# A layer with 32 experts: token columns copied in SBUF by index in place of row gathers from DRAM, the residual kept in DRAM meanwhile

## The chip, the cores and the metric

One core of one Trainium2 chip runs the whole kernel. The metric is the device time of one execution in microseconds (us), the median of several runs. Matrix work is on TensorE (PE), element-wise work on VectorE (DVE) and ScalarE (ACT), GpSimd (POOL) issues indirect DMAs, and SyncE (SP) issues most of the other DMAs.

## The reference

One layer on x of 512 tokens by 1024 channels: a token mixer (stick-breaking attention and retention), cross-attention into 256 memory rows, a mixture of experts, and a last RMSNorm. The change lies in the mixture:

```python
logits = h @ w_router + b_router            # h = rmsnorm(x, g_moe), 512 x 1024
top_val, top_idx = lax.top_k(logits, 4)     # 4 of 32 experts for each token
gate = softmax(top_val)
# for each expert e and each of its tokens
hc  = h[token] @ w1[e] + b1[e]              # 1024 -> 2048
act = min(hc_glu, 7) * sigmoid(1.702 * ...) * (clip(hc_lin) + 1)
y   = act @ w2[e] + b2[e]                   # 1024 -> 1024
x[token] += gate * y
```

An expert's weights are 12 MB in float32, those of all 32 experts 384 MB. All of them are read once.

## The kernel before

**Up to the experts** the kernel runs projections, attention, retention and cross-attention. It ends with `res`, the residual stream of 512 tokens (`work` columns 8192 to 12288, 2 MB), and `h_nat`, its normalised rows with tokens on partitions. ACT stores `h_nat` into the DRAM tensor `h_rows` (`row_store`, L1007). The router's result is ranked on DVE, and PE runs idle matmuls meanwhile (`keep_running`, L1901).

**The experts** are taken in the order of their token counts, large and small alternating, from a table `order` in SBUF. A turn treats groups of 32 tokens: 3 groups (96 tokens) for experts 0, 1 and the even ones, 2 groups (64) for the odd ones (`CYCLE = (3, 2)`). An expert that has more tokens than that gets an overflow pass at the end, which these inputs do not use. The weights come in chunks of 1 MB, 12 for an expert: 8 for the first product (`up`, L1983) and 4 for the second (`down`, L2009). They go round 20 slots of SBUF. SP issues the load of a chunk (L530) as soon as PE has used the chunk that is in its slot (`w_used`), so SP is up to 20 chunks ahead.

The input of an expert must have channels on partitions (`x_t`). For expert 0 PE builds it with selection matrices from `h_nat` (L2076). For expert n from 1 on the steps are these:

- DVE compares the slots of all tokens with the table of places (`choose`, L1395), PE turns that into row numbers (`index`, L1920), and DVE writes them as integers (`idx`, L1426).
- POOL gathers the rows of `h_rows` by an indirect DMA into `xrows` (`gather_rows`, L687), 96 or 64 rows of 4 KB.
- PE transposes them (`x_turn`, L1941), and ACT copies the result out of PSUM (`x_keep`, L1031).

The order in a turn of PE is written out by hand:

```python
up(p, ...); x_turn(p + 1); spread(p - 1, ...); index(p + 2, ...); down(p - 1, ...); act_turn(p, ...)
```

DVE does `swiglu(p)` (L1526, L1530), waits for the gather `x_in`, and does `index`, `choose` and `now`. ACT does `gate_silu(p)` (L1039), `x_keep(p + 1)`, `y_evict(p - 1)` (L1051, L1052) and `act_keep(p)` (L1044). POOL scatters the outputs of an expert into the DRAM tensor `y_tok` (L726), 3 or 2 indirect DMAs of quarter rows.

**At the end** SP loads the 16 tiles of `y_tok` (L584), DVE adds them to `res` with the gates (L1580), and the last RMSNorm follows.

## Time and profile before

| | |
|---|---|
| median of 3 runs | 1755.39 us (1753.14 to 1755.88) |
| the profiled execution | 1752.49 us |
| its span on the core | 1750.8 us |
| mean granted clock of TensorE | 0.994 |
| PE busy | 1663.0 us (95%) |
| DVE busy | 451.3 us (26%) |
| ACT busy | 379.0 us (22%) |
| POOL busy | 184.9 us (11%) |
| read from HBM, written | 485.59 MB, 22.94 MB |
| queue q1 (SP's, weights) | 469.79 MB |
| queue q0 (POOL's) | 34.59 MB |

Busy time is the union of an engine's instructions; register and DMA-issuing instructions are not in it. A DMA share is the mean busy share of the core's 16 DMA engines in a stretch, and the GB/s are what they moved. The queue lines give packets, MB and the share of the 16 engines' time that the packets took. In a timeline each row has its start, its duration, the engine and line, the tile written and the tile read, the count, and in brackets how long the engine was idle before it and for what.

### The profile page before, as it was taken

Reading aid. Unit: us, or ns where it says so; the run is one execution under the profiler, and the core shown is the slowest. Engines: PE = TensorE matmul, PEld = TensorE weight load, DVE = VectorE, ACT = ScalarE, POOL = GpSimd, SP = SyncE. Lnnn points to the kernel's source line nnn. Section 1 sums busy time; section 2 is a strip of 40 time slices with the busy share of each in tenths; the row PEclk is TensorE's granted clock in tenths of the full one; section 3 lists DMA queues with packets and bytes.
Section 4 is the critical chain, followed back from the end, with each engine's and each line's share of the span. In section 5 each row is a group of like instructions: output and inputs, shape, how many; then the busy total and the mean of one; then the engine's idle time right before and its main releaser. Section 6 shows DMA issues by size and latency. Waiting matters only on the chain.

```text
span 1750.8 us, 36491 instructions
## 1 busy us (share of the span) xinstructions
PE 1663.0 (95%) x15752; PEld 936.6 (53%) x15752; DVE 451.3 (26%) x933; ACT 379.0 (22%) x596; POOL 184.9 (11%) x269
## 2 busy tenths in 40 slices
PE   7989999999999999999999999989899889899995
PEld 6766887888888867434344434424334334334331
DVE  4354526424645253521000100001001000010005
ACT  5564233433335333000000000000001000000001
POOL 0011301000000010011111111101101101111110
PEclk9999999999999999999999999999999999999999
DMA  7103634234225425799999999999999999999997
GB/s 257 61 25 91 219 124 160 73 96 168 97 74 203 180 81 218 310 372 391 398 411 401 408 399 410 401 412 409 404 411 406 405 412 403 409 411 402 413 415 286
DMA packets 98706, 508.71 MB, mean 291 GB/s; under 512 B 10650, under 2 KB 10834, under 8 KB 49056
## 3 DMA queue, kind: packets, MB, share of 16 engines
q1 hardware_dynamic: 86224, 469.79, 68.1%
q0 software_dynamic: 11760, 34.59, 6.0%
q8 instruction: 126, 2.06, 0.5%
q10 hardware_dynamic: 576, 2.10, 0.3%
q14 instruction: 20, 0.16, 0.0%
HBM read 485.59 MB, written 22.94 MB: 290 GB/s over the span
## 4 chain that ended last, share of the span: by engine, by line
PE 63%; SPq 19%; DMA 11%; issue 3%; DVE 3%; ACT 1%; POOL 0%; ACTq 0%; DVEq 0%; POOLq 0%
SPq L530 18%; PE ps L1983 15%; PE ps L1656 10%; PE ps L1657 10%; PE ps L1658 10%; PE ps L2009 8%; DMA moe<-in_w_exp_in 3%; DMA ring<-in_w_exp_in 3%; DMA ring<-in_w_exp_out 2%; PE ps L1752 1%; DMA ring<-y_tok 1%; PE ps L1799 1%; PE ps L1819 1%; PE ps L509 1%; PE ps L1941 1%
## 5 line engine op out<-in xcount | busy, mean ns | idle before, releaser
L1983 PE MATMUL ps<-ring,moe 128*32 128x512 f32 x3104 | 348.7, 597 | 23.8 <-DMA ring<-in_w_exp_in 23.8
L1526 DVE TENSOR_SCALAR moe<-ps 128x768 f32<-128x768 f32 (+1 forms) x32 | 26.7, 833 | 845.8 <-PE ps L1983 845.8
L1983 PEld LDWEIGHTS ps<-ring,moe 128*32 128x32 f32 x3104 | 92.6, 110 | 263.4 <-issue 202.6
L1122 DVE TENSOR_TENSOR wl<-raw,wh 128x1024 fp32r<-128x1024 f32 x102 | 123.6, 1224 | 230.1 <-ACT wh L787 230.1
L2009 PE MATMUL ps<-ring,moe 128*32 128x256 f32 x3136 | 174.0, 379 | 0.4 <-DMA ring<-in_w_exp_out 0.3
L1039 ACT ACTIVATE moe<-ps 128x768 f32<-128x768 f32 (+1 forms) x32 | 22.8, 711 | 641.8 <-DVE moe L1526 641.8
L1656 PE MATMUL ps<-oph,wh 128*128 128x512 f32 x384 | 151.1, 394 | 4.6 <-DVE opl L1157 2.2
L787 ACT ACTIVATE wh<-raw 128x1024 fp32r<-128x1024 f32 x102 | 106.8, 1061 | 222.5 <-PE ps L1658 222.5
L1657 PE MATMUL ps<-opl,wh 128*128 128x512 f32 x384 | 149.8, 390 | 0.0
L1658 PE MATMUL ps<-oph,wl 128*128 128x512 f32 x384 | 149.8, 390 | 0.0
L2009 PEld LDWEIGHTS ps<-ring,moe 128*32 128x32 f32 x3136 | 93.5, 110 | 71.5 <-DMA ring<-in_w_exp_out 1.5
L1983 PE MATMUL ps<-moe 128*32 128x512 f32 x1056 | 119.7, 593 | 7.8 <-DMA moe<-in_w_exp_in 7.7
L1983 PE MATMUL ps<-work,moe 128*32 128x512 f32 x1024 | 115.2, 594 | 11.0 <-DMA work<-in_w_exp_in 11.0
L726 POOL DMA_INDIRECT y_tok<-moe,spare x79 | 78.8, 997 | 256.8 <-ACT moe L1052 222.6
L1656 PE MATMUL ps<-wh,oph 128*128 128x512 f32 x248 | 97.5, 393 | 0.7 <-ACT work L845 0.7
L1657 PE MATMUL ps<-wl,oph 128*128 128x512 f32 x248 | 96.6, 389 | 0.0
L1658 PE MATMUL ps<-wh,opl 128*128 128x512 f32 x248 | 96.5, 389 | 0.0
L1656 PEld LDWEIGHTS ps<-oph,wh 128*128 128x128 f32 x384 | 72.4, 188 | 21.8 <-issue 6.0
L695 POOL CAST sel_c<-work 96x32 bf16 (+1 forms) x64 | 20.7, 349 | 581.8 <-DVE moe L1426 547.2
L1658 PEld LDWEIGHTS ps<-oph,wl 128*128 128x128 f32 x384 | 72.3, 188 | 15.3
L1983 PEld LDWEIGHTS ps<-moe 128*32 128x32 f32 x1056 | 31.1, 110 | 92.2 <-issue 69.6
L1657 PEld LDWEIGHTS ps<-opl,wh 128*128 128x128 f32 x384 | 72.4, 189 | 14.5
(302 smaller groups left out, 1811.1 us busy)
## 6 DMA issues: line engine op xcount, KB each, us to landing
ring<-in_w_exp_in SPq DMA_DIRECT2D x152, 1024.0 KB, 28.3
ring<-in_w_exp_out SPq DMA_DIRECT2D x78, 1024.0 KB, 29.2
moe<-in_w_exp_in SPq DMA_DIRECT2D x52, 1024.0 KB, 28.6
work<-in_w_exp_in SPq DMA_DIRECT2D x52, 1024.0 KB, 29.0
moe<-in_w_exp_out SPq DMA_DIRECT2D x26, 1024.0 KB, 28.2
raw<-in_w_in SPq DMA_DIRECT2D x25, 1024.0 KB, 5.4
work<-in_w_exp_out SPq DMA_DIRECT2D x24, 1024.0 KB, 28.3
y_tok<-spare POOLq DMA_DIRECT2D x16, 512.0 KB, 4.2
```

The lines of the kernel that those rows point to most:

```text
L530: sp.dma_start(held(s), expert_chunk(e, c)).then_inc(w_ring[s], 16)
L695: nc.gpsimd.tensor_copy(dst, exp_rows[0:96, bass.ds(e, 1)].to_broadcast([96, 32])).then_inc(sel_ready, 1)
L726: pool.indirect_dma_start(out=y_parts, out_offset=bass.IndirectOffsetOnAxis(ap=place_now[:, j:j + 1], axis=0), in_=y_sb[:, j, :], in_offse ...
L787: nc.scalar.activation(half_hi(g), raw[:, c % RAW, g % 2 * PC:(g % 2 + 1) * PC], ACT.Copy).then_inc(w_hi, 1)
L1039: nc.scalar.activation(glu_s[:, 0:g], ps[:, 0:g, 0:256].rearrange("p j (n a) -> p j a n", a=2), ACT.Silu, scale=ALPHA).then_inc(s_ready, 1)
L1122: nc.vector.tensor_tensor(half_lo(g), raw[:, g // 2 % RAW, g % 2 * PC:(g % 2 + 1) * PC], half_hi(g), ALU.subtract).then_inc(w_lo, 1)
L1526: nc.vector.tensor_scalar(act_n[:, 0:g], ps[:, 0:g, 256:512].rearrange("p j (n a) -> p j a n", a=2), 1.0 - LIMIT, 1.0 + LIMIT, ALU.max, AL ...
L1656: nc.tensor.matmul(o, a_hi_, b_hi_, start=start, stop=False)
L1657: nc.tensor.matmul(o, a_hi_, b_lo_, start=False, stop=False)
L1658: return nc.tensor.matmul(o, a_lo_, b_hi_, start=False, stop=stop)
L1983: ins = nc.tensor.matmul(ps[32 * s:32 * s + 32, j, :], xt[:, k, 32 * j:32 * j + 32], w[:, s, :, :], start=False, stop=(k == KT - 1), tile_ ...
L2009: ins = nc.tensor.matmul(y_bank(s, j), at[:, a, j, q, :], w[:, a, s, :], start=False, stop=(q == W2 - 1 and a == 1), tile_position=(0, 32 ...
```

## The change

Four things change.

1. **Columns instead of rows.** PE transposes all of `h_nat` (`column_turn`, 8 times 4 transposes), ACT copies the result to `h_cols`, 8 x 512 columns in the place of `res` (`column_tile`). For experts 2 to 31 `index` gets 8 more matmuls on PE, which give the token numbers as a row on one partition, and DVE writes them to `tok_row` (2 buffers). DVE then copies the first half of the columns and ACT the second half, one instruction for a token with a register in its address, 8 registers loaded at a time (`copy_tokens`). `x_t` has two buffers, so the copies for expert p+2 are made in turn p.
2. **Gone** for experts 2 to 31: the gather, `x_turn`, `x_keep`, and DVE's wait for `x_in`. Expert 1 keeps them.
3. **The residual waits in DRAM.** SP stores `res` into `r_rows` in two halves of 1 MB among the first weight loads, and loads it back (2 MB) after the last weight load, ahead of the tiles of `y_tok`. ACT waits for both stores before it writes `h_cols`; DVE waits for the load before its first sum.
4. **Idle matmuls gone.** The two `keep_running` calls (24 matmuls) make way for the 32 transposes. The last 8 of them wait until ACT has copied the first four tiles, and `index(0)` waits for all eight tiles.

```diff
@@ copy_tokens, new
+        def x_t(g, b):
+            return m_(1024 - 1024 * b, KT * 32 * g).rearrange("p (k n) -> p k n", k=KT)
+        h_cols = w_(8192, KT * T).rearrange("p (k n) -> p k n", k=KT)
+        def copy_tokens(engine, copy, n, lo, hi):
+            b = n % 2
+            for s in range(lo, hi, 8):
+                _, tokens = nc.values_load_multi_w_load_instructions(
+                    tok_row[b][:, s:s + 8], engines=[engine], min_val=0, max_val=T - 1,
+                    skip_runtime_bounds_check_because="the row is clamped to the last token when it is written")
+                for i, token in enumerate(tokens):
+                    ins = copy(x_t(CYCLE[b], b)[:, :, s + i:s + i + 1], h_cols[:, :, bass.ds(token, 1)])
+            return ins
@@ SP
+                if s in (13, 15):
+                    half = (s - 13) // 2
+                    sp.wait_ge(tile_out["dve"], slabs[f"co{half}"].out0 + 4)
+                    sp.dma_start(r_rows[:, :, 512 * half:512 * half + 512], res[:, :, 512 * half:512 * half + 512]).then_inc(res_moved, 16)
...
             load(final, EC - 1, (CHUNKS - 1) % SLOTS)
+            sp.wait_ge(x_dve, NE - 2)
+            sp.wait_ge(x_act, NE - 2)
+            sp.dma_start(res, r_rows).then_inc(res_moved, 16)
@@ POOL
-            def step(p, old, e, g):
-                pool.wait_ge(xt_made, p + 2)
-                pool.wait_ge(idx_out, p + 2)
+            def step(p, i, old, e):
+                pool.wait_ge(row_ready, p + 1)
                 pool.wait_ge(sel_used, p + 1)
                 pool.sem_inc(bias_turn, 1)
                 bias_on(old, e)
-                gather_rows(g)
@@ ACT
+            act.wait_ge(res_moved, 32)
+            for k in range(KT - 2):
+                column_tile(k)
             act.preload_act_table_set("natural_log_exp_and_others")
...
+            for k in range(KT - 2, KT):
+                column_tile(k)
...
-            def step(p, m, i):
+            def step(p, m, i, more=True):
                 gate_silu(p, CYCLE[i])
-                x_keep(p + 1, CYCLE[1 - i])
                 y_evict(p - 1, CYCLE[i - 1], p * EC + (DOWNS - EC))
                 act_keep(p, CYCLE[i])
+                if more:
+                    act.wait_ge(row_ready, p + 1)
+                    act.sem_inc(bias_turn, 1)
+                    copy_tokens(mybir.EngineType.Activation, lambda out, in_: nc.scalar.activation(out, in_, ACT.Copy), i,
+                                16 * CYCLE[i], 32 * CYCLE[i]).then_inc(x_act, 1)
@@ DVE
                 swiglu(p, CYCLE[i], p * EC + UPS)
-                dve.wait_ge(x_in, p * 16 + 16)
-                index(p + 2, CYCLE[i], i)
+                index(p + 2, CYCLE[i], i, row=True)
                 e = expert_at(p + 3)
                 choose_with(e, e, CYCLE[1 - i])
                 now(p - 1, g, stores)
+                copy_part(p + 2, i)
@@ PE
-            keep_running(18)
+            pe.wait_ge(nat_ready, TT)
+            for k in range(KT - 2):
+                column_turn(k)
...
+                    for t in range(TT):
+                        for c in range(2):
+                            nc.tensor.matmul(ps[0:1, 3, 64:64 + 32 * g], column[:, t, c, 0:1], pick[:, t, 0:32 * g],
+                                             start=(t == 0 and c == 0), stop=(t == TT - 1 and c == 1), skip_group_check=True)
...
-            keep_running(6)
+            pe.wait_ge(ht_out, KT + 4)
+            for k in range(KT - 2, KT):
+                column_turn(k)
...
+                    pe.wait_ge(x_dve, n - 1)
+                    pe.wait_ge(x_act, n - 1)
...
                 up(p, CYCLE[i], p * 2 + 1)
-                x_turn(p + 1)
                 spread(p - 1, groups(p - 1), p - 1, p + 2, (p + 1) % 2)
                 if to_index:
-                    index(p + 2, CYCLE[i])
+                    index(p + 2, CYCLE[i], row=True)
                 down(p - 1, groups(p - 1), p * 2)
-                act_turn(p, CYCLE[i], p + 2)
+                act_turn(p, CYCLE[i])
```

The lists below are the built program's instructions in their order. This is PE between the products of two experts, before:

```order
L1983 MATMUL ps<-work,moe 32x512 x48
L1941 MATMUL ps<-ident,moe 128x96 x8
L1930 MATMUL ps<-spare,ident 32x2 x8
L1920 MATMUL ps<-spare,moe 96x2 x12
L2000 MATMUL ps<-bias_b,sel_c 32x256 x8
L2009 MATMUL ps<-ring,moe 32x256 x32
L2009 MATMUL ps<-moe 32x256 x32
L1951 MATMUL ps<-ident,moe 128x128 x6
```

and the same place in the changed kernel:

```order
L2056 MATMUL ps<-work,moe 32x512 x48
L2056 MATMUL ps<-ring,moe 32x512 x24
L2056 MATMUL ps<-moe 32x512 x24
L1996 MATMUL ps<-spare,ident 32x2 x8
L1982 MATMUL ps<-moe,spare 1x96 x8
L1986 MATMUL ps<-spare,moe 96x2 x12
L2073 MATMUL ps<-bias_b,sel_c 32x256 x8
L2082 MATMUL ps<-ring,moe 32x256 x64
L2020 MATMUL ps<-ident,moe 128x128 x6
```

The eight transposes of gathered rows (L1941) are gone; eight matmuls with one output row (L1982) stand ahead of the twelve of `index` (L1986).

This is ACT in one turn of an expert with 3 groups, before:

```order
L1039 ACTIVATE moe<-ps 128x768
L1031 ACTIVATE moe<-ps 128x768
L1051 ACTIVATE moe<-ps 128x256
L1052 ACTIVATE moe<-ps 128x512
L1044 ACTIVATE moe<-ps 128x768
```

and now, with the first columns of its half:

```order
L1076 ACTIVATE moe<-ps 128x768
L1088 ACTIVATE moe<-ps 128x256
L1089 ACTIVATE moe<-ps 128x512
L1081 ACTIVATE moe<-ps 128x768
L523 TENSOR_LOAD moe
L1063 ISA
L1063 ACTIVATE moe<-work 128x8
L1063 ISA
L1063 ACTIVATE moe<-work 128x8
```

`x_keep` (L1031) is gone. Behind `act_keep` (L1081) stands one register load for eight columns (L523), and for each column an instruction on registers (ISA) and the copy of 8 elements on 128 partitions (L1063); with 3 groups ACT has 6 such loads and 48 copies, with 2 groups 4 and 32. DVE has as many.

This is SP before the experts in the changed kernel, where the two stores of the residual (L569) stand:

```order
L547 DMA ring<-in_w_exp_in 128x2048 [waits w_used]
L547 DMA ring<-in_w_exp_in 128x2048
L569 DMA r_rows<-work 128x4x512 [waits tile_out_dve]
L547 DMA moe<-in_w_exp_in 128x2048 [waits w_used]
L547 DMA moe<-in_w_exp_in 128x2048
L569 DMA r_rows<-work 128x4x512 [waits tile_out_dve]
L547 DMA work<-in_w_exp_out 128x2048 [waits lg_done,nat_ready]
L547 DMA work<-in_w_exp_out 128x2048
L547 DMA work<-in_w_exp_out 128x2048 [waits xt_made,h_stored]
```

The first store stands behind the second load of a pair, the other behind the last load whose slot the projections held; the loads with "waits xt_made,h_stored" follow.

## Rows read from the trace of the kernel before

**Rows 1.** The page, part 2: busy tenths of the DMA engines in 40 slices.

```profile
DMA  7103634234225425799999999999999999999997
```

**Rows 2.** Timeline of PE (start, duration, engine, line, tiles): the starts of four even experts.

```profile
836.72 0.83 PE L1974 MATMUL ps<-bias_b,sel_c 96*32 96x512 bf16 x12
...
1070.06 0.83 PE L1974 MATMUL ps<-bias_b,sel_c 96*32 96x512 bf16 x12
...
1129.25 0.83 PE L1974 MATMUL ps<-bias_b,sel_c 96*32 96x512 bf16 x12
...
1648.91 0.83 PE L1974 MATMUL ps<-bias_b,sel_c 96*32 96x512 bf16 x12
```

**Rows 3.** Timeline of PE in two turns: a wait inside up, and x_turn.

```profile
1302.20 1.92 PE L1983 MATMUL ps<-ring,moe 128*32 128x512 f32 x16 [0.69 <-DMA ring<-in_w_exp_in]
...
1346.43 0.88 PE L1941 MATMUL ps<-ident,moe 96*128 96x96 f32 x8
```

**Rows 4.** DMA queues in 1465 to 1480 us: packets, MB, share of 16 engines.

```profile
q1 hardware_dynamic: 866, 6.30, 101.0%
```

**Rows 5.** Timeline of POOL from 1480 us: the gathers of one pair.

```profile
1480.69 1.01 POOL L687 DMA_INDIRECT moe<-h_rows,moe  x1 [0.27 <-issue]
...
1511.07 0.99 POOL L687 DMA_INDIRECT moe<-h_rows,moe  x1 [0.15 <-issue]
```

**Rows 6.** DMA queues in 1515 to 1521 us, a gather for 64 rows landing.

```profile
q1 hardware_dynamic: 259, 1.90, 88.6%
q0 software_dynamic: 80, 0.21, 11.9%
```

**Rows 7.** DMA queues in 1484 to 1491 us, a gather for 96 rows landing.

```profile
q1 hardware_dynamic: 306, 2.22, 88.2%
q0 software_dynamic: 112, 0.28, 13.0%
```

**Rows 8.** DMA queues in 1524 to 1533 us, three scatters landing.

```profile
q1 hardware_dynamic: 473, 3.46, 92.1%
```

**Rows 9.** DMA queues in 1129.25 to 1648.91 us, eight pairs of experts.

```profile
q8 instruction: 49, 0.80, 0.6%
...
moe<-h_rows,moe POOLq DMA_INDIRECT x16
```

**Rows 10.** Stretches of time: busy of each engine, granted clock, DMA share, GB/s.

```profile
685.00:690.00 5.00, 5.00 (x27) 4.20 (x26) 2.62 (x4) 2.17 (x6) 0.00 (x0) 1.00 0.00 0
740.00:745.00 5.00, 5.00 (x40) 1.47 (x36) 4.86 (x5) 0.00 (x0) 0.00 (x0) 0.78 1.03 362
760.00:770.00 10.00, 10.00 (x196) 5.64 (x192) 2.78 (x8) 1.51 (x2) 1.71 (x3) 1.00 0.89 320
```

**Rows 11.** Timeline of all engines where the experts begin.

```profile
689.45 0.80 SPq L530 DMA_DIRECT2D moe<-in_w_exp_in  x2
...
695.73 0.60 ACT L1016 ACTIVATE work<-ps 128x512 f32<-128x512 f32 x1 [1.14 <-PE ps L1885]
...
703.95 7.38 PE L2076 MATMUL ps<-moe,work 128*128 128x96 f32 x64
...
711.37 0.81 ACT L1031 ACTIVATE moe<-ps 128x768 f32<-128x768 f32 x1 [9.87 <-PE ps L2076]
...
716.48 0.16 DVE L1463 CAST work<-moe 1x15 uint32<-1x15 f32 x1
...
721.13 0.96 SPq L530 DMA_DIRECT2D ring<-in_w_exp_in  x2
```

**Rows 12.** Timeline of ACT and DVE: short instructions, and a register load ahead of one.

```profile
691.55 0.21 ACT L1003 ACTIVATE small<-small 128x4 f32<-128x4 f32 x1 [0.65 <-DVE small L1354]
...
1349.56 0.15 DVE L1429 COPY spare<-ps 96x2 f32<-96x2 f32 x1
...
1721.73 1.28 ACT L1097 ACT_TABLE_LOAD   x1 [0.20 <-issue]
```

**Rows 13.** Timeline at the end: the sums wait for the expert rows.

```profile
1720.32 5.48 DVE L1580 SCALAR_TENSOR_TENSOR work<-ring,work 128x1024 f32<-128x1024 f32 x4 [6.93 <-DMA ring<-y_tok]
```

More of the change, by code:

```diff
@@ L429, in layer_kernel @@
         zero_x = sem("zero_x")
+        res_moved = sem("res_moved")
+        row_ready, x_dve, x_act = (sem(n) for n in ("row_ready", "x_dve", "x_act"))
         pickl_ready, gl_made, gl_kept, own_done = (
@@ L1024, in _, with copy_part, x_keep @@
                 ins.then_inc(gate_exp, 1)
+            for k in range(KT - 2, KT):
+                column_tile(k)
             act.preload_act_table_set("silu_and_others")
-            def x_keep(n, g):
-                act.wait_ge(xt_made, n + 1)
-                nc.scalar.activation(x_t(g).rearrange("p (b k) n -> p b k n", b=2),
+            def copy_part(n, b):
+                act.wait_ge(row_ready, n - 1)
+                copy_tokens(mybir.EngineType.Activation, lambda out, in_: nc.scalar.activation(out, in_, ACT.Copy), b,
+                            16 * CYCLE[b], 32 * CYCLE[b]).then_inc(x_act, 1)
+            def x_keep(made, g, b):
+                act.wait_ge(xt_made, made)
+                nc.scalar.activation(x_t(g, b).rearrange("p (b k) n -> p b k n", b=2),
                                      ps[:, 6:8, 0:4 * CAP].rearrange("p b (k n) -> p b k n", k=4)[:, :, :, 0:32 * g], ACT.Copy).then_inc(xt_kept, 1)
@@ L1086, in _ @@
                     step(m * 2 + (2 + i), m, i)
-            step(NE - 2, CYCLES - 1, 0)
+            step(NE - 2, CYCLES - 1, 0, more=False)
             last_step(NE - 1)
@@ L1933, in spread, with x_turn @@
                 ins.then_inc(spread_done, 1)
-            def x_turn(n, first=False):
-                pe.wait_ge(x_in, n * 16)
-                if not first:
-                    pe.wait_ge(at_kept, n - 1)
+            def x_turn(landed, kept=None):
+                pe.wait_ge(x_in, landed * 16)
+                if kept is not None:
+                    pe.wait_ge(at_kept, kept)
                 for k in range(KT):
@@ L1943, in x_turn, with act_turn @@
                 ins.then_inc(xt_made, 1)
-            def act_turn(n, g, after):
+            def act_turn(n, g, after=None):
                 pe.wait_ge(act_ready, n + 1)
-                pe.wait_ge(xt_kept, after)
+                if after is not None:
+                    pe.wait_ge(xt_kept, after)
+                else:
+                    pe.wait_ge(at_kept, n)
                 for h in range(2):
@@ L1963, in chunk_in, with up @@
                 return held(c)
-            def up(n, g, sel, first=False, over=None, between={}):
-                pe.wait_ge(xt_kept, n + 1)
+            def up(n, g, sel, first=False, over=None, between={}, kept=None):
+                if kept is not None:
+                    pe.wait_ge(xt_kept, kept)
+                else:
+                    pe.wait_ge(x_dve, n - 1)
+                    pe.wait_ge(x_act, n - 1)
                 if not first:
@@ L1977, in up @@
                     ins.then_inc(sel_used, 1)
-                xt = x_t(g)
+                xt = x_t(g, 0 if over is not None else n % 2)
                 for k in range(KT):
@@ L2079, in _ @@
             pe.wait_ge(b_hi, 3)
+            pe.wait_ge(ht_out, 2 * KT)
             index(0, groups(0))
-            up(0, groups(0), 1, first=True, between={1: lambda: index(1, groups(1))})
-            x_turn(1, first=True)
-            index(2, CYCLE[0])
+            up(0, groups(0), 1, first=True, between={1: lambda: index(1, groups(1))}, kept=1)
+            x_turn(1)
+            index(2, CYCLE[0], row=True)
             act_turn(0, groups(0), 2)
-            up(1, groups(1), 3)
-            x_turn(2)
+            up(1, groups(1), 3, kept=2)
             spread(0, groups(0), 0, 3, 0)
-            index(3, CYCLE[1])
+            index(3, CYCLE[1], row=True)
             down(0, groups(0), 2, first=True)
-            act_turn(1, groups(1), 3)
+            act_turn(1, groups(1))
             def step(p, i, to_index=True):
                 up(p, CYCLE[i], p * 2 + 1)
-                x_turn(p + 1)
                 spread(p - 1, groups(p - 1), p - 1, p + 2, (p + 1) % 2)
                 if to_index:
-                    index(p + 2, CYCLE[i])
+                    index(p + 2, CYCLE[i], row=True)
                 down(p - 1, groups(p - 1), p * 2)
-                act_turn(p, CYCLE[i], p + 2)
+                act_turn(p, CYCLE[i])
             for p in range(2, NE - 2):
@@ L2108, in _ @@
             up(NE - 1, CYCLE[1], 2 * NE - 1)
-            act_turn(NE - 1, CYCLE[1], NE)
+            act_turn(NE - 1, CYCLE[1])
             last_down()
@@ L2121, in _ @@
                         spread(j + NE, GR, j + (NE - 1), j + (NE + 1), 0, 2)
-                        x_turn(j + NE)
-                        up(j + NE, GR, j * 2 + (2 * NE + 1), over=j)
-                        act_turn(j + NE, GR, j + (NE + 1))
+                        x_turn(j + 2, j + (NE - 1))
+                        up(j + NE, GR, j * 2 + (2 * NE + 1), over=j, kept=j + 3)
+                        act_turn(j + NE, GR, j + 3)
                         down(j + NE, GR, j * 2 + (2 * NE + 2), over=j)
```

70 lines of the change are left out of this document (45 added, 25 removed).

## The prediction, made before any run of the changed kernel

> **What bounds the kernel now.** I read the page first. From slice 18 of 40 on, where the experts are under way, the DMA engines stand at nine tenths or more but for the last slice [rows 1]. So the question is whether PE or the weight stream sets the pace. The timeline of PE answers it in two parts. The even experts start at 836.72 and, four pairs on, at 1070.06 us: 58.3 us a pair, with PE never idle. From 1129.25 to 1648.91 us eight pairs pass: 65.0 us a pair [rows 2], and inside `up` PE waits some 0.6 us for nearly every chunk [rows 3]. A pair of experts reads 24 chunks of 1.049 MB, 25.17 MB. The DMA engines move this at their full share all the time; at first PE lives on the 20 chunks that were loaded ahead and eats this lead at 6.7 us a pair, then it goes at the stream's pace. The bound is the DMA stream. PE has 6.7 us of slack in each pair.
>
> What does the stream do with its time? Where nothing but weights moves, q1 gets 6.30 MB through in 15 us, 0.420 MB/us [rows 4]. At this rate 24 chunks take 59.9 us, and a pair takes 65.0. The missing 5.1 us are what POOL's indirect DMAs and the instruction fetch take. The change removes one of the two indirect kinds, the gathers.
>
> **The gathers, removed.** POOL issues one in each turn [rows 5]; its rows land some 4 to 10 us later. In the 6 us of a gather of 64 rows q1 moves 1.90 MB where 2.52 would go: 0.62 MB less, 1.5 us [rows 6]. In the 7 us of one of 96 rows it moves 2.22 of 2.94 MB, 1.7 us less [rows 7]. The gathered bytes alone are 0.21 and 0.28 MB, 0.5 and 0.7 us, so more than their bytes is lost: q1's share falls to 88.6% while its bytes fall to 75% of what the clean rate gives. The mean is 1.6 us a gather, 3.2 us a pair. As a cross-check, three scatters cost 3.78 - 3.46 = 0.32 MB, 0.8 us [rows 8]; two I put at 0.5; the fetch is 0.6% of 65.0, 0.4 us [rows 9]. Of the 5.1 us this leaves 3.4 for the two gathers, 1.7 each.
>
> There are 30 such gathers (16 in the eight pairs, [rows 9]). The two for experts 2 and 3 fall in a stretch in which the stream is short of free slots anyway: between 760 and 770 us the DMA share is 0.89 [rows 10]. Their removal gives nothing. The other 28 give 28 x 1.6 = 44.8 us. In the first pairs a turn with 3 groups frees slots more slowly than the emptier queue fills them, so a little goes unused: I take off 3 us by choice (0 to 10). **Gain: 42 us.**
>
> Does PE let it through? The new pair takes 65.0 - 3.2 = 61.8 us, against 58.3 of PE. PE also loses `x_turn`, 0.88 us a turn [rows 3], and gets 8 matmuls with one output row, which I put between nothing and that same row of 8 matmuls; they even out at worst. PE's own chain from 836.72 would reach expert 30, 13 pairs on, at 1595; the stream brings it there at 1648.91 - 42 = 1607. PE stays hidden, by 12 us: the end of the experts is still the stream's.
>
> **The copies on DVE and ACT, added.** Each engine copies 48 and 32 columns in a pair, with 10 loads of 8 registers. No row shows such a copy. From below: the shortest ACT instruction here takes 0.21 us, two DVE copies of a few elements start 0.06 to 0.07 us apart and take 0.15, and a register load ahead of ACT's table load leaves 0.20 us idle [rows 12]. So ACT needs 48 x 0.21 + 6 x 0.20 = 11 us for the large expert, DVE less. From above: six single register loads of SP lie between DVE's 716.64 us (716.48 + 0.16) and SP's first refill at 721.13 [rows 11], 0.75 us each. If each of the 8 registers cost that, a column would cost 0.96 us. I take 0.21 to 0.30 us a column, as a load of eight is one instruction; the nearest row is ACT's own. ACT's copies start behind `act_keep(p)`, beside `up(p+1)`. `gate_silu(p+1)` stands behind them, and it is needed before `act_turn(p+1)`, which comes after `up(p+1)` and `down(p)`: eight chunks of 2 groups at 1.92 us [rows 3] are 15 us, and `down(p)` with 3 groups is a good sixth of PE's pair of 58.3 us, 10 us: 25 us in all. 48 columns fit up to 0.5 us each. The products `up(p+2)` that need them come a whole turn later. Cost: 0. If the cover goes, the price is that of the rival below.
>
> A page has a price for the loads. The Trainium skill, "Runtime: NRT & Kernel Launch", Instruction fetch mechanics, states that a TENSOR_LOAD takes about 200 ns for each register even in bulk; by that a column costs 0.41 us, 48 of them 20 us, still under the cover, and the sum is unchanged. No row here shows a load of eight.
>
> DVE's and ACT's longer programs are fetched too: some 350 instructions a pair beside PE's 1600 or so, at a total fetch share of 0.6% now [rows 9]. I put 1 us on it (0 to 2).
>
> **The start, moved.** The first store of `res` goes out where the DMA engines stand still: share 0.00 from 685 to 690 us [rows 10]. Free. The second goes behind the two loads of 689.45 us [rows 11]: 2.1 MB, 5 us; itself 1.05 MB, 2.5 us; and ACT's own stores of `h_rows` share the engines from 693 us on. I expect it landed near 702 (698 to 705). ACT waits for that behind its copy of 695.73 us, while PE's ranking and DVE do not. Then ACT copies six tiles at 0.6 us, loads its table, does the gates (2 us), two tiles, a table of 1.28 us: 10 us, so it is ready for `x_keep(0)` near 712, against 711.37 now. PE's last 8 transposes wait for four tiles (704.5), so the product of expert 0 begins near 706 in place of 703.95 and takes 7.4 us [rows 11]. Both put the first `up` 1 to 3 us later, and with it the table of the order and the first refill. As the stream runs dry there already, this passes on in full: +3 us (0 to 5). The idle matmuls are gone: after a stop of PE the granted clock reads 0.78 in 740 to 745 us [rows 10]; a like dip over the product of expert 0 costs +1 us (0 to 3).
>
> **The end, moved.** The load of `res`, 2.1 MB, goes in between the last weights and the tiles of `y_tok` in the same queue. The engines are full there, and DVE's first sum waits 6.93 us for such a tile at 1720.32 us [rows 13]. So all tiles come 2.1/0.42 = 5 us later: +5 us (4 to 6).
>
> **The sum.** -42 + 1 + 3 + 1 + 5 = -32 us. The profiled execution took 1752.5 us, so 1720.5; the median of the runs, 2.9 us above it, goes to **1723.4 us**. Its own bounds: with 1.7 us a gather, nothing lost early and the small ends of the rest 47.6 - 4 = 43.6 us less, 1711.8; with 1.4 us a gather, 10 lost early and the large ends 29.2 - 16 = 13 us less, 1742.
>
> **The rivals.**
>
> *A gather costs its bytes only.* The dips of q1 in [rows 6, 7] would then come from something else that stands in the same place. Its 0.245 MB at 0.42 MB/us are 0.58 us, 28 of them 16 us; with the 10 us of the other terms the gain is 6 us: 1749. For it: a row is 4 KB, long against the other packets. Against it: three scatters, with as many bytes and smaller pieces, lose 0.8 us together, about their bytes, in windows that differ only in what POOL sent. The Trainium skill, "DMA: Bandwidth & Descriptors", Specifications, gives 512 bytes as the least transfer at line rate; by that rule a gathered row of 4 KB costs its bytes and this rival holds. The trace disagrees with it here, 1.5 us against 0.5.
>
> *The copies become the bound, and the kernel is slower.* The place is ACT between `act_keep(p)` and `gate_silu(p+1)`. ACT's work in a pair is 80 columns and some 4 us of its other copies. Once a column costs more than (65.0 - 4)/80 = 0.76 us, ACT takes longer than the pair does now and PE waits for `act_ready` and `x_act`. At the upper price of 0.96 us a pair takes 81 us, 16 more, over 14 pairs 224: with the other terms about 1990. Against it: no short instruction on ACT takes a third of this. For it: the price of a register load in eights, and of an address that waits for it, is not in the trace.
>
> *The change does not free the stream.* If SP's issuing rather than the engines limited q1, the weights would not move up. The terms at start and end would stay: 1765. Against it: the share is 101.0% with weights alone [rows 4].
>
> **How the numbers follow.** Forecast 0.78, bytes only 0.11, copies bound 0.07, stream not freed 0.04. A measurement of this kernel can tell 0.2%, 3.5 us. Bytes only is mostly faster (1749) and partly no change. Faster 0.87, same 0.03, slower 0.10. The range is the forecast's own, 1711 to 1742; what lies outside is the three rivals, 0.22, less the better half of the first, which may reach into it.
>
> **What would show it.** Right: pairs of 61 to 62.5 us late in the experts, q1 near 0.42 MB/us but for the scatters; ACT's copies at 0.2 to 0.3 us and idle before `gate_silu`; the first refill at 721 to 726 us; the tiles of `y_tok` 5 us later behind the weights. Wrong: late pairs near 64 (bytes only), PE waiting for ACT or DVE at `up` or `act_turn` (copies bound), or a first refill after 730 us.

## The result, and the profile after

| | before | after |
|---|---|---|
| median | 1755.45 us (1753.14 to 1755.88, 4 runs) | 1723.4 us (1720.73 to 1726.49, 4 runs) |
| profiled execution, span | 1752.49, 1750.8 us | 1724.01, 1722.2 us |
| read from HBM, written | 485.59, 22.94 MB | 477.86, 25.03 MB |
| queue q0 (POOL's) | 34.59 MB | 26.70 MB |
| DVE, ACT busy | 451.3, 379.0 us | 613.2, 510.4 us |

The ratio of after to before is 0.9821, interval 0.9802 to 0.9840: 32 us less, where 32 were forecast.

The page of the changed kernel, part 2 (40 slices of 43 us) and part 3 (queue, packets, MB, share of 16 engines):

```profile
GB/s 249 74 25 61 228 125 173 89 98 159 86 98 192 199 3 243 248 386 369 412 418 420 419 421 419 420 419 420 419 420 419 420 420 419 420 420 418 419 402 263
...
q1 hardware_dynamic: 87808, 473.99, 68.7%
q0 software_dynamic: 8880, 26.70, 4.6%
...
q14 instruction: 29, 0.24, 0.0%
```

From slice 21 to slice 38 the engines now move 418 to 421 GB/s without a dip. The timeline of PE shows the starts of even experts (start us, duration, engine, line, tiles), the same matmuls as [rows 2]:

```profile
840.87 0.83 PE L2047 MATMUL ps<-bias_b,sel_c 96*32 96x512 bf16 x12
...
1069.87 0.83 PE L2047 MATMUL ps<-bias_b,sel_c 96*32 96x512 bf16 x12
...
1304.22 0.83 PE L2047 MATMUL ps<-bias_b,sel_c 96*32 96x512 bf16 x12
...
1427.49 0.83 PE L2047 MATMUL ps<-bias_b,sel_c 96*32 96x512 bf16 x12
...
1489.92 0.83 PE L2047 MATMUL ps<-bias_b,sel_c 96*32 96x512 bf16 x12
...
1614.02 0.83 PE L2047 MATMUL ps<-bias_b,sel_c 96*32 96x512 bf16 x12
```

The early pairs take (1069.87 - 840.87)/4 = 57.25 us, PE's own pace (58.3 before). For the late ones the same five pairs are compared, those that end with expert 30. In the kernel before they begin here:

```profile
1324.48 0.83 PE L1974 MATMUL ps<-bias_b,sel_c 96*32 96x512 bf16 x12
```

They take (1614.02 - 1304.22)/5 = 61.96 us now and took (1648.91 - 1324.48)/5 = 64.89 before. Expert 30 starts 34.9 us earlier than before. The queues in one late pair, of 62.43 us:

```profile
q1 hardware_dynamic: 3514, 25.58, 98.6%
q0 software_dynamic: 240, 0.51, 2.1%
q8 instruction: 6, 0.10, 0.6%
```

And in 15 us with hardly anything but weights (1470 to 1485 us), beside [rows 4]:

```profile
q1 hardware_dynamic: 858, 6.24, 100.4%
```

ACT in a large turn (timeline; in brackets the idle time before the row and for what). The copies come in eights, with one load of 8 registers between:

```profile
1459.05 0.96 ACT L1108 ACTIVATE moe<-work 128x8 f32 x8
1460.48 0.97 ACT L1108 ACTIVATE moe<-work 128x8 f32 x8 [0.46 <-issue]
...
1466.28 0.97 ACT L1108 ACTIVATE moe<-work 128x8 f32 x8 [0.46 <-issue]
1478.53 0.60 ACT L1076 ACTIVATE moe<-ps 128x512 f32<-128x512 f32 x1 [11.27 <-DVE moe L1572]
```

DVE likewise:

```profile
1454.86 1.06 DVE L527 COPY moe<-work 128x8 f32 x8 [0.58 <-issue]
```

An octet and its load take (0.97 + 0.46)/8 = 0.18 us a column on ACT and (1.06 + 0.58)/8 = 0.205 us on DVE. `gate_silu` (L1076) waits 11.27 us for DVE's result with ACT idle: the copies stand in nobody's way.

The start, in the timelines of all engines, beside [rows 11]:

```profile
690.20 0.81 SPq L547 DMA_DIRECT2D moe<-in_w_exp_in  x2
...
691.42 0.38 SPq L569 DMA_DIRECT2D r_rows<-work  x1
...
705.52 3.05 ACT L1044 ACTIVATE work<-ps 128x512 f32<-128x512 f32 x6 [8.44 <-DMA r_rows<-work]
...
707.64 1.97 PE L1957 MATMUL ps<-ident,work 128*128 128x128 f32 x8 [4.48 <-ACT work L1044]
709.40 8.10 PE L2150 MATMUL ps<-moe,work 128*128 128x96 f32 x64
...
717.54 0.81 ACT L1068 ACTIVATE moe<-ps 128x768 f32<-128x768 f32 x1 [4.16 <-PE ps L2150]
...
727.65 0.61 SPq L547 DMA_DIRECT2D ring<-in_w_exp_in  x2
```

ACT stands 8.44 us for the second store, PE 4.48 us for ACT, and the product of expert 0 takes 8.10 us in place of 7.38. The windows (busy time of each engine, granted clock, DMA share, GB/s) show why the latter, and what it costs the stream:

```profile
705.00:710.00 5.00, 2.36 (x12) 2.36 (x12) 4.64 (x9) 4.45 (x8) 0.00 (x0) 0.50 1.03 431
710.00:715.00 5.00, 5.00 (x42) 5.00 (x41) 0.00 (x0) 3.36 (x11) 0.00 (x0) 0.89 0.08 33
715.00:720.00 5.00, 4.60 (x59) 3.58 (x61) 1.93 (x5) 0.81 (x1) 0.95 (x1) 1.00 0.29 69
```

PE was stopped, and the granted clock reads 0.50 (1.2 of 2.4 GHz) at first and 1.00 from 715 us. The DMA engines meanwhile have nothing to do (0.08 and 0.29): all slots are full and the first refill waits for PE. It comes at 727.65 us against 721.13 before.

The end, the loads of SP and the first sum of DVE, beside [rows 13]:

```profile
1657.49 2.13 SPq L604 DMA_DIRECT2D work<-r_rows  x1
...
1667.03 29.13 SPq L608 DMA_DIRECT2D ring<-y_tok  x16
...
1690.32 1.28 DVE L1631 SCALAR_TENSOR_TENSOR work<-ring,work 128x1024 f32<-128x1024 f32 x1 [12.30 <-DMA ring<-y_tok]
```

From expert 30's start to the end of the span pass 1722.2 - 1614.02 = 108.2 us, against 1750.8 - 1648.91 = 101.9 before: 6.3 more. The first sum of DVE starts 76.3 us after expert 30, against 71.4 before: 4.9 of the 6.3. The other 1.4 come behind it. PE adds some tiles of `y_tok` with their gates, 8 matmuls for a tile of tokens. Here are the first 8 before, then the same 8 in the changed kernel, for which DVE waits:

```profile
1725.58 3.70 PE L2055 MATMUL ps<-ring,moe 128*128 128x512 f32 x8 [2.01 <-DMA ring<-y_tok]
```

```profile
1696.21 6.05 PE L2128 MATMUL ps<-ring,moe 128*128 128x512 f32 x8 [5.04 <-DMA ring<-y_tok]
...
1702.29 1.23 DVE L1643 TENSOR_TENSOR work<-ps,work 128x1024 f32<-128x1024 f32 x1 [0.87 <-PE ps L2128]
```

PE had waited 5.04 us, and the granted clock reads 0.50 from 1695 to 1700 us; in the kernel before it waited 2.01 us and the clock reads 1.00 from 1722 to 1732 us. So 0.87 of the 1.4 us belong to the clock.

### The profile page after: what moved, and what is told of

It reads as the page before. It is cut to its first block, busy times and chain, and to the rows that moved or that the text cites. A ratio compares the mean times of both kernels' runs of the same rounds, so it can differ in the third digit from the quotient of the medians.

```text
span 1722.2 us, 41426 instructions
## 1 busy us (share of the span) xinstructions
PE 1645.5 (96%) x15736; PEld 933.0 (54%) x15736; DVE 613.2 (36%) x2133; ACT 510.4 (30%) x1774; POOL 151.4 (9%) x239
## 3 DMA queue, kind: packets, MB, share of 16 engines
q0 software_dynamic: 8880, 26.70, 4.6%
HBM read 477.86 MB, written 25.03 MB: 292 GB/s over the span
## 4 chain that ended last, share of the span: by engine, by line
PE 69%; SPq 17%; DMA 8%; issue 3%; DVE 2%; ACT 1%; POOL 0%; POOLq 0%; DVEq 0%; ACTq 0%
PE ps L2056 18%; SPq L547 16%; PE ps L1708 10%; PE ps L1709 10%; PE ps L1710 10%; PE ps L2082 10%; DMA moe<-in_w_exp_out 2%; DMA ring<-in_w_exp_in 2%; DMA moe<-in_w_exp_in 2%; PE ps L1804 1%; DMA ring<-y_tok 1%; PE ps L1851 1%; PE ps L1871 1%; DMA r_rows<-work 1%; PE ps L515 1%
## 5 line engine op out<-in xcount | busy, mean ns | idle before, releaser
L2056 PEld LDWEIGHTS ps<-ring,moe 128*32 128x32 f32 x3104 | 94.5, 110 | 245.6 <-issue 205.7
L527 DVE COPY moe<-work 128x8 f32 x1200 | 161.6, 178 | 82.4 <-issue 81.5
L1108 ACT ACTIVATE moe<-work 128x8 f32 x1072 | 131.6, 205 | 53.0 <-issue 53.0
L1076 ACT ACTIVATE moe<-ps 128x768 f32<-128x768 f32 (+1 forms) x32 | 22.7, 711 | 411.7 <-DVE moe L1572 411.7
L2082 PEld LDWEIGHTS ps<-ring,moe 128*32 128x32 f32 x3136 | 95.2, 110 | 70.1 <-issue 1.4
```

The lines of the kernel that those rows point to most:

```text
L527: ins = copy(x_t(CYCLE[b], b)[:, :, s + i:s + i + 1], h_cols[:, :, bass.ds(token, 1)])
L1108: copy_tokens(mybir.EngineType.Activation, lambda out, in_: nc.scalar.activation(out, in_, ACT.Copy), i, 16 * CYCLE[i], 32 * CYCLE[i]).the ...
L2056: ins = nc.tensor.matmul(ps[32 * s:32 * s + 32, j, :], xt[:, k, 32 * j:32 * j + 32], w[:, s, :, :], start=False, stop=(k == KT - 1), tile_ ...
L2082: ins = nc.tensor.matmul(y_bank(s, j), at[:, a, j, q, :], w[:, a, s, :], start=False, stop=(q == W2 - 1 and a == 1), tile_position=(0, 32 ...
```

## The experiments

Beside these runs the kernel before had medians of 1754.0 to 1755.5 us. Differences below are between medians, unless said otherwise.

### The gathers

**The gathers back, into other partitions.** The 28 gathers of experts 4 to 31 are issued in POOL's order as before; nobody uses the rows. DVE writes the row numbers for them again and waits for each gather, as it did before.

```diff
@@ POOL, in the step of a turn
+                    pool.wait_ge(idx_out, p + 2)
...
+                    pool.indirect_dma_start(out=spare[32:32 + 32 * CYCLE[i], 0:D], out_offset=None, in_=h_rows,
+                                            in_offset=bass.IndirectOffsetOnAxis(ap=idx[0:32 * CYCLE[i], :], axis=0),
+                                            bounds_check=T - 1, oob_is_err=False).then_inc(x_in, 16)
```

> The changed kernel, and POOL also gathers the rows of experts 4 to 31 as before, into an unused part of SBUF; nobody uses them. Theory (a gather takes 1.6 us of the weight stream, more than its bytes): 28 gathers give back about 42 us, so near 1765 us, and late pairs of experts go back from 62 to 65 us. Rival (a gather costs its bytes, 0.58 us): 16 us, near 1739 us, pairs of 63 us. Rival (the gain came from the shorter PE turn without the 8 transposes): no change from 1723 us.

Measured: 1750.16 us (1747.9 to 1752.88), ratio to before 0.9978 (0.9968 to 0.9987), 26.8 us above the changed kernel: 0.96 us a gather, between the two theories. The rival that the gain came from the shorter turn of PE falls, since PE's turn is as short as in the changed kernel.

**The kernel before without its gathers.**

```diff
-                gather_rows(g)
...
-                pe.wait_ge(x_in, n * 16)
+                pe.wait_ge(x_in, 16)
...
```

DVE's waits for `x_in` are lowered in the same way.

> The kernel before, without the gathers of experts 2 to 31; the transposes stay and take the rows of expert 1 each time, so these experts compute on wrong tokens. Theory: the stream's gain alone, without the costs at start and end: 42 us less than before, near 1713 us, pairs of 62 us. Rival (bytes only): 16 us less, near 1739 us.

Measured: 1714.45 us, ratio 0.9777 (0.9761 to 0.9793), 39.6 us below the kernel before that was measured beside it; expert 30 starts at 1611.31. The forecast's first term was 42. The transposes of PE stand here as before, so the whole gain comes from the gathers, and the other parts of the change give some 9 us of it back (1723.4 against 1714.45). By the trace of the changed kernel start and end cost more, 12.8 us; here the first `up` itself starts 2.0 us later than before (714.28), and the other 2 us are not explained.

**Plain rows in place of gathers.** The same number of rows of `h_rows`, without an index.

```diff
-                gather_rows(g)
+                pool.dma_start(xrows[0:32 * g, :], h_rows[0:32 * g, :]).then_inc(x_in, 16)
```

> The kernel before, but each gather for experts 2 to 31 is a plain DMA on the same queue of the first 96 or 64 rows of h_rows into the same place: the same bytes, the same row length, the same target, no index; these experts compute on wrong tokens. If the loss of the weight stream lies in the shape (rows of 4 KB into single partitions), it stays: near 1755 us. If it lies in the indexed DMA itself, only the bytes are left: 28 times 1.0 us less, near 1729 us.

Measured: 1765.08 us, ratio 1.0064 (1.0047 to 1.0081): 11 us slower than with the gathers. q0 moves 36.53 MB in place of 34.59, since a gather leaves out the rows of empty places. The index is not what costs.

**The gathers back, into the partitions of before.** The first two experiments left a contradiction: the same 28 gathers are worth 39.6 us in the kernel before and 26.8 in the changed one. One difference is where the rows land: partitions 0 to 95 and 0 to 63 before, 32 to 127 and 32 to 95 in the first experiment.

```diff
@@ against the first experiment
-                    pool.indirect_dma_start(out=spare[32:32 + 32 * CYCLE[i], 0:D], out_offset=None, in_=h_rows,
+                    pool.indirect_dma_start(out=spare[0:32 * CYCLE[i], 0:D], out_offset=None, in_=h_rows,
```

> The changed kernel with the 28 gathers of experts 4 to 31 back in POOL's order, as in the run that cost 26.8 us, but with their rows put into partitions 0 to 95 or 0 to 63, as before, and not into 32 to 127 or 32 to 95. Theory (the partitions decide how much a gather costs, and the 1.5 us each that the change won came with the low ones): about 40 us slower than the changed kernel, 1763, and more weight packets of 0.65 us than in that run. Rival (the partitions do not matter; a gather in this place costs 0.95 us): 1748 to 1752.

Measured: 1763.4 us (1762.95 to 1766.62), ratio 1.0058 (1.0043 to 1.0074). 40.0 us above the changed kernel, as the theory has it: 1.43 us a gather, and 13 us more than with the other partitions. The DMA queues show which gathers differ. All windows are 8 us long. First the experiment with partitions from 32 up: without a gather (1430 to 1438 us), with one of 96 rows (1412 to 1420), with one of 64 rows (1441 to 1449):

```profile
q1 hardware_dynamic: 464, 3.38, 101.3%
```

```profile
q1 hardware_dynamic: 363, 2.64, 89.5%
q0 software_dynamic: 112, 0.28, 11.1%
```

```profile
q1 hardware_dynamic: 420, 3.06, 92.5%
q0 software_dynamic: 80, 0.22, 6.9%
```

And the experiment with partitions from 0 up, a gather of 64 rows (1451 to 1459 us):

```profile
q1 hardware_dynamic: 378, 2.74, 91.6%
q0 software_dynamic: 80, 0.22, 9.3%
```

At 3.38 MB in 8 us (0.4225 MB/us) the 96 rows take 0.74 MB from the weights, 1.75 us. 64 rows into partitions 0 to 63 take 0.64 MB, 1.5 us; 64 rows into 32 to 95 take 0.32 MB, 0.76 us, not far above the 0.22 MB of their own. The single packets say it more sharply. A weight packet of 8192 bytes takes 0.31 us. Counted over the trace's packets, while a gather of 96 rows lands or one of 64 rows into partitions 0 to 63, mostly 60 to 100 of them take over 0.4 us, in the kernel before as in this one. While 64 rows land in partitions 32 to 95, 0 to 2 do, in all 14 such gathers. A scatter, which reads SBUF, has 0 to 3 late in the experts.

The windows are a little high. Over the five last pairs the run from partition 32 up takes (1641.13 - 1321.09)/5 = 64.01 us and the one from 0 up (1653.63 - 1329.38)/5 = 64.85, which is 2.05 and 2.89 us above the changed kernel, where the windows add up to 2.5 and 3.25. The difference between the two runs, 0.84 us a pair, is near the windows' 0.75.

So the partitions are shown to set the price of a gather of 64 rows: the two kernels differ in this one line. For 96 rows both places, 0 to 95 and 32 to 127, cost the same 1.75 us, and that their excess has the same cause is argued and not shown. The Trainium skill, "SBUF — State Buffer", SBUF: two separate sides (the DMA port swizzle), has a rule that fits: of SBUF's 16 DMA ports, partitions 0 to 63 reach eight and 64 to 127 the other eight. By it 64 rows from partition 0 all press on one half, 96 rows load the halves 64 to 32 from either end, and only 32 to 95 is even; it says nothing of the weights beside them, but the trace agrees in all four cases. An estimate by it: 64 rows of 4 KB through half of 0.42 MB/us are 0.26/0.21 = 1.25 us, evenly 0.62; the windows show 1.5 and 0.76. For 96 rows the fuller half has 64 too, so by this estimate they cost 1.25 as well, while the windows show 1.75. An even split of 96 rows (48 and 48) was not tried.

### The start and the end

**No store of `res`.** `x` is loaded at the end in place of the stored residual.

```diff
-                if s in (13, 15):
-                    half = (s - 13) // 2
-                    sp.wait_ge(tile_out["dve"], slabs[f"co{half}"].out0 + 4)
-                    sp.dma_start(r_rows[:, :, 512 * half:512 * half + 512], res[:, :, 512 * half:512 * half + 512]).then_inc(res_moved, 16)
...
-            act.wait_ge(res_moved, 32)
-            sp.dma_start(res, r_rows).then_inc(res_moved, 16)
+            sp.dma_start(res, x[0].rearrange("(t p) d -> p t d", p=P)).then_inc(res_moved, 16)
```

> The changed kernel without the two stores of the residual and without ACT's wait for them; at the end x is loaded in the residual's place (the same 2 MB), so the output lacks the mixer's and the attention's part. Theory: the wait for the second store costs some 5.4 us at the start of the experts and passes on in full: near 1718 us, first refill near 722 us in place of 727.7, and no fall of TensorE's granted clock at the product of expert 0. Rival (the stream's lead hides a late start): within 1 us of 1723.

Measured: 1720.39 us (1718.56 to 1720.41), 3.0 less, with the first refill at 723.51 us. PE's product starts at 705.99 and takes 7.38 us again; the weight loads ahead of it were issued 1.29 us later than in the changed kernel (691.49 against 690.20), a drift from before the experts. Taken from that issue on, the first `up` starts 22.8 us later without the stores (714.27) and 28.2 us with them (718.40). The stores cost 5.4 us at this place; the drift of 1.29 us and another 1.1 us are missing in the total.

**The second store by tiles, ahead of two weight loads.**

```diff
-                if s in (13, 15):
...
+                if s == 13:
+                    sp.wait_ge(tile_out["dve"], slabs["co0"].out0 + 4)
+                    sp.dma_start(r_rows[:, :, 0:512], res[:, :, 0:512]).then_inc(res_moved, 16)
+                    for t in range(TT):
+                        sp.wait_ge(tile_out["dve"], slabs["co1"].out0 + t + 1)
+                        sp.dma_start(r_rows[:, t, 512:D], res[:, t, 512:D]).then_inc(res_moved, 16)
```

> The changed kernel, but the second store of the residual goes out tile by tile as each is done, and ahead of the two weight loads that stood before it. Theory: the stores land near 695 us in place of 705, ACT waits for nothing, the first product comes 5 to 6 us earlier and so does the end: near 1718 us. Rival (the stores only push the h_rows stores and the weights back): no change.

Measured: 1718.85 us (1717.23 to 1720.57), 4.6 less: nearly all that the stores cost. The product starts at 704.39 us with full clock.

**No load of `res` at the end.**

```diff
-            sp.dma_start(res, r_rows).then_inc(res_moved, 16)
```

> The changed kernel without the load of the residual at the end: the last sums add to whatever stands in its place, so the residual is missing from the output. Theory: 2 MB less in a full queue ahead of the tiles of y_tok: 5 us less, near 1718 us. Rival (the tiles wait for the last scatter anyway): no change.

Measured: 1717.87 us (1713.79 to 1718.54), 5.5 less; 5 were put on it.

**The load in four tiles among the tiles of `y_tok`.**

```diff
-            sp.dma_start(res, r_rows).then_inc(res_moved, 16)
+            sp.dma_start(res[:, 0, :], r_rows[:, 0, :]).then_inc(in_x[0], 16)
             for u in range(TT * TOPK):
+                if u in (4, 8, 12):
+                    sp.dma_start(res[:, u // 4, :], r_rows[:, u // 4, :]).then_inc(in_x[u // 4], 16)
```

> The changed kernel, but the residual is loaded back in four tiles, each just ahead of the four tiles of y_tok that it is summed with. Theory: the first sum can begin 3.7 us earlier, since only 0.5 MB stands before its first tile in place of 2 MB, and DVE's chain from there is as long as before: 3 us less, near 1720 us. Rival (the chain on DVE and PE waits for the later tiles instead): 0 to 1 us.

Measured: 1721.75 us (1721.1 to 1725.06), 1.7 less where the theory has 3. The first sum starts at 1686.72 us, 3.6 us earlier as foreseen, but the later sums wait for their tiles, one of them 2.47 us at 1696.07, which is the rival's mechanism. The times of this run and of the changed kernel overlap, so the 1.7 us by themselves are inconclusive.

**Both.** The early store and the load by tiles together, with the lines of the two diffs above.

> The changed kernel with both edits of the residual's way: the second half of the store by tiles and ahead of two loads of weights, and the reload in four tiles between the tiles of y_tok. Theory (the start and the end add up): the 4.6 us of the first edit and the 1.7 us of the second, about 6 us less than the changed kernel, 1717. Rival (the start comes early only to lose at the end, since the stream still sets the time of expert 30 and of the reload): no more than the first edit alone, 1719.

Measured: 1716.28 us (1715.1 to 1717.98), ratio to before 0.9785 (0.9772 to 0.9799), 7.1 less than the changed kernel; by the ratios, 0.0036 of 1755, 6.3 us. The first `up` starts at 713.10, expert 30 at 1609.14, 4.9 us earlier, and from there to the end of the span (1714.6) pass 105.5 us in place of 108.2. Start and end add up. Of the kernels here that copy the tokens this is the fastest.

### The copies

**All columns on ACT.** This was to test whether the split matters, with ACT twice as busy and still covered.

```diff
-                            16 * CYCLE[b], 32 * CYCLE[b]).then_inc(x_act, 1)
+                            0, 32 * CYCLE[b]).then_inc(x_act, 1)
...
-                copy_tokens(mybir.EngineType.DVE, nc.vector.tensor_copy, b, 0, 16 * CYCLE[b]).then_inc(x_dve, 1)
+                dve.sem_inc(x_dve, 1)
```

> The changed kernel, but ACT copies all columns and DVE none. At 0.18 us a column ACT needs 17 us for a large expert and 11.5 for a small one, 29 of 62 us in a pair. Theory (25 us of cover behind act_keep): no change from 1723 us. Rival (the halves were needed): PE waits at act_turn or up, pairs over 62 us.

Measured: 1751.56 us (1748.52 to 1754.1, 10 runs), 28 more than the changed kernel. The theory fell, though its reasoning about ACT held. The timeline of ACT, large turn:

```profile
1368.02 0.96 ACT L1108 ACTIVATE moe<-work 128x8 f32 x8 [0.46 <-issue]
1372.29 0.60 ACT L1076 ACTIVATE moe<-ps 128x512 f32<-128x512 f32 x1 [3.30 <-DVE moe L1572]
```

ACT is done 3.30 us before it is needed. PE waits for weights. The page, part 2, and the queues of one pair (1319.3 to 1383.7 us):

```profile
GB/s 245 73 25 76 232 125 160 72 97 168 90 80 193 192 70 232 289 371 390 418 418 419 418 419 418 419 415 405 417 404 407 412 390 400 406 397 394 406 370 222
```

```profile
q1 hardware_dynamic: 3499, 25.48, 97.6%
q0 software_dynamic: 240, 0.53, 2.1%
q8 instruction: 6, 0.10, 0.7%
q14 instruction: 5, 0.04, 0.1%
```

The stream itself is slower from slice 27 on, pairs take (1577.20 - 1190.85)/6 = 64.4 us, and a queue that is silent in the changed kernel moves 5 packets of 8 KB of instructions in each pair. Two runs were to tell what did it.

**ACT's loop only made longer.** The split of the change, but waits that are met at once ahead of the copies.

```diff
+                    for _ in range(16 * CYCLE[i] * 9 // 4):
+                        act.wait_ge(w_first, 16)
                     copy_tokens(mybir.EngineType.Activation, lambda out, in_: nc.scalar.activation(out, in_, ACT.Copy), i,
```

> The changed kernel with its own split of the columns; ACT's loop body only made longer, by 108 and 72 waits on a semaphore that was raised long before (180 instructions a pair, about what the 80 further columns added in the run with all on ACT). They read no tensor and load no register. Theory (the length of the body costs, since its instructions are brought again in each round): ACT's instruction queue moves some 80 to 90 packets in place of 29, late pairs take over 63.5 us, about 1750 us. Rival (the 80 further register loads and copies themselves disturb the stream, the length does not): 29 packets or few more, late pairs at 62, 1722 to 1727 us.

Measured: 1750.72 us (1749.8 to 1752.35, 10 runs), 27.3 more. The page, part 2, and the same stretch:

```profile
GB/s 245 73 25 80 230 124 160 72 97 168 97 73 196 189 73 233 273 382 392 419 418 418 419 418 419 419 414 407 416 402 408 405 395 403 406 396 407 405 376 215
```

```profile
q14 instruction: 5, 0.04, 0.2%
```

Slice by slice this is nearly the run with all columns on ACT. The waits read no tensor and load no register, so neither is needed for the loss; longer code in ACT's loop is enough. The waits also take time: the copies of a large turn begin some 4 us later behind `act_keep` than in the changed kernel. No run separates this delay from the length of the code, but PE waits for nothing except weights here too.

**All columns on DVE.**

```diff
-                copy_tokens(mybir.EngineType.Activation, lambda out, in_: nc.scalar.activation(out, in_, ACT.Copy), b,
-                            16 * CYCLE[b], 32 * CYCLE[b]).then_inc(x_act, 1)
+                act.sem_inc(x_act, 1)
...
-                copy_tokens(mybir.EngineType.DVE, nc.vector.tensor_copy, b, 0, 16 * CYCLE[b]).then_inc(x_dve, 1)
+                copy_tokens(mybir.EngineType.DVE, nc.vector.tensor_copy, b, 0, 32 * CYCLE[b]).then_inc(x_dve, 1)
```

> The changed kernel, but DVE copies all columns of an expert and ACT none: the mirror of the run with all on ACT, which cost 28 us though ACT fitted. It tells whether that cost belongs to a long loop body or to ACT. Theory (a loop body that has grown by two instructions a column, 80 columns a pair, and a load per eight, is brought from DRAM again in every round, and these reads slow the weight packets): DVE's body grows by the same number, its instruction queue moves more packets than now, some weight packets take about 0.65 us in place of 0.31, late pairs take 63.5 to 65 us, about 1750 us. Rival (the cost is ACT's alone): late pairs stay at 62 and the time at 1722 to 1728. The copies themselves, 80 more columns of 0.205 us in a pair, are 16 us a pair and fit in DVE's idle time by both.

Measured: 1773.34 us (1770.95 to 1776.98), ratio 1.0117 (1.0102 to 1.0133), 50 more. Its page:

```profile
q14 instruction: 85, 0.70, 0.1%
```

So it is not ACT's alone, and PE again waits for nothing but weights. With nearly the same number of packets as on ACT the cost is almost double, and pairs take (1596.69 - 1198.70)/6 = 66.3 us; the theory had 1750. What a longer loop costs on which engine is measured here; why the price differs is open.

## Why the prediction was right, point by point

- **The gathers, 42 us.** Expert 30 came 34.9 us earlier although the stream started 6.5 us later, 41.4 us by the stream. Without gathers the kernel before gained 39.6, and 28 gathers put back cost 40.0. The mechanism was right: a gather takes about three times its bytes from the stream. The price was read a little high. Five late pairs are 64.89 - 61.96 = 2.93 us shorter each, 1.47 a gather where the windows gave 1.6, and 28 x 1.47 is 41. The 3 us that were taken off by choice for the first pairs made up for it, and that is luck. The cause, which the prediction left open, is for 64 rows the partitions that they are written to.
- **The rival that a gather costs its bytes** falls, with its 1749 us. It comes near for one kind, 64 rows into partitions 32 to 95, which the kernel before does not have. The Trainium skill, "DMA: Bandwidth & Descriptors", Specifications, gives 512 bytes as the least transfer at line rate. That is no guide to the price here: 64 rows of 4 KB cost 1.4 times their bytes (0.32 for 0.22 MB) or 2.9 times (0.64), by their partitions.
- **PE hidden.** PE was put at 58.3 us a pair and 12 us of cover. It took 57.25: `x_turn` went, 1.76 us a pair, and the row matmuls took back 1.76 - 1.08 = 0.7. From 840.87 us PE's chain would reach expert 30 at 840.87 + 13 x 57.25 = 1585, so the cover was 29 us.
- **The copies, 0.** 0.18 us a column on ACT and 0.205 on DVE, below the 0.21 to 0.30 that were taken. The rival in which the copies bound falls: it began at 0.76. The Trainium skill, "Runtime: NRT & Kernel Launch", Instruction fetch mechanics, gives 200 ns for each register, and the trace does not agree for eights from SBUF: the load of 8 registers leaves 0.46 us idle on ACT and 0.58 on DVE, some 0.06 to 0.07 a register.
- **The instruction fetch, 1 us** for the longer programs: in the changed kernel the share stayed at 0.6% of q8 and q14 was silent, so it cost nothing that can be seen. But this term was sized by bytes, and that is the weak step of the prediction: had the copies all stood on one engine, it would have been 28 or 50 us. That the halves keep both loops short was luck to the forecast.
- **The start, 3 + 1 us,** was sized too low: 6.5 (727.65 against 721.13), outside the 721 to 726 that were named. The step that was off is the landing of the second store. It was put at 702, which left some 4 us for sharing the engines with ACT's stores of `h_rows`, and it ended just before ACT's first copy at 705.52, at the late end of 698 to 705. From 698 to 706 us ACT's stores (queue q10) moved 1.84 MB and q1 only 1.50. From there the prediction's own chain holds: PE's product 4 us behind the landing, 709.40 us in place of 706. The lower clock on the product cost 0.7 where 1 was put. From the issue of the loads (690.20 against 689.45) on it is 5.8 us, and the experiments give the stores 5.4 of it: 4.7 of waiting and 0.7 of the lower clock.
- **The end, 5 us:** 6.3 by the trace, 5.5 by the experiment without the load. The first sum comes 4.9 us later, as forecast. The prediction looked for a fall of the clock at the start alone; the second one, at the end, makes up 0.9 of the rest.
- **The sum.** -41.4 + 6.5 + 6.3 = -28.6 us, and the two profiled executions stand 1752.49 - 1724.01 = 28.5 apart, where the prediction had 32: start and end cost 2.5 and 1.3 us more than they were given, the gathers brought 0.6 less, the fetch took back its 1. The profiled execution of before lies 3.0 us below its median and that of after 0.6 above, so the medians are 32 apart. So the profiled execution was missed by 3.5 us (1720.5 against 1724.01), and that the forecast meets the median to a tenth is chance. The mechanism is shown, and each term is within 2.5 us.

## What to carry to other kernels

When a DMA stream at full rate is the bound, the price of another transfer is what the stream loses while it lands, read over a window of the queue's bytes, and here it was up to three times the transfer's own bytes. For 64 rows, moving them to the partitions 32 to 95 halved it; try that before removing the transfer. Count the instructions of a loop body too: the longer bodies here showed as packets in every round on an instruction queue that was silent before, and as a slower stream, not as a wait for that engine. When an engine's wait is moved into a serial start, follow it to the engine that waits for it in turn, and to the clock that this engine loses.

## What the runs showed of the hardware that was not expected

- 64 rows of 4 KB into partitions 32 to 95 cost the weight stream 0.76 us, into 0 to 63 1.5 us; 28 gathers moved by 32 partitions, 13 us of the whole.
- ACT's loop body longer by 180 waits: 27.3 us of 1723, with 5 packets of 8 KB (0.04 MB) more in each pair. At 0.42 MB/us these are 0.1 us a pair, while the pair takes 64.4 - 62 = 2.4 us more. The weight packets of 8192 bytes are the ones that slow down (from 1319.3 to 1383.7 us 69 of 3086 take over 0.4 us, and 6 of 3223 in the changed kernel), mostly not at the time of the instruction packets. The packets come in every pair from about 910 us on, but the stream slows only from about 1140 us, so such packets alone do not slow it. How the two hang together is open.
- In the changed kernel q14 has no packet between 907 and 1570 us, some 11 pairs, though ACT and DVE go round their loops: they need nothing new. In the runs with the longer bodies it has 5 packets in every pair. The other instruction queue, q8, brings 6 packets of 16 KB in every pair in all of them. The Trainium skill, "Runtime: NRT & Kernel Launch", Instruction fetch mechanics, says that an engine holds a window of two blocks of instructions and that a taken branch out of it forces a fetch. The trace agrees, with the packets in every round of the longer bodies and none in 11 pairs of the shorter ones; how many instructions such a window holds no run here tests.
- PE's granted clock reads 0.50 from 1695 to 1700 us, behind a wait of 5.04 us for a tile of `y_tok`, and 8 matmuls take 6.05 us in place of 3.70. A load that is moved into the end of a kernel costs its bytes and, in this case, 0.87 us of waiting for PE besides.
